# A chunked recurrence laid out by head parity: products in two opposite corners of the TensorE array

## What is computed

```python
def step(state, inp):
    r_t, w_t, k_t, v_t, a_t, b_t = inp
    sa = jnp.einsum('bhij,bhj->bhi', state, a_t)
    state = state * w_t[:, :, None, :] + sa[..., None] * b_t[:, :, None, :] + v_t[..., :, None] * k_t[:, :, None, :]
    y = jnp.einsum('bhij,bhj->bhi', state, r_t)
    return state, y
...
y = (y - mean) * lax.rsqrt(var + GN_EPS) * ln_w + ln_b
y = y + jnp.sum(rh * kh * r_k, axis=-1, keepdims=True) * vh
```

## Time and profile before

| | |
|---|---|
| median of the runs | 1049.82 us |
| span of the profiled execution | 1047.7 us |
| TensorE busy | 831.4 us (79%) |
| VectorE busy | 644.8 us (62%) |
| ScalarE busy | 390.1 us (37%) |
| GpSimd busy | 343.9 us (33%) |
| share of the chain that ended last | PE 50%, DMA 27%, DVE 12%, issue 5% |
| L880, the inversion's products | 864 records, 21.8 us busy |
| L954, L974, L984, L990 | 64 records each, 4.6, 4.6, 4.4 and 4.5 us busy |
| L964, products with the state | 48 records, 6.5 us busy |
| L873, gram products | 128 records, 4.5 us busy |

### The profile page before, as it was taken

One profiled execution on the slowest core, in us unless ns is written; L12 is line 12 of the kernel. 1 busy time (PEld: TensorE's weight loads), 2 busy tenths in 40 slices (PEclk: granted clock), 3 DMA queues, 4 the chain that ended last, 5 costly groups with the idle time before them and its releaser, 6 DMA issues.

```text
span 1047.7 us, 16371 instructions
## 1 busy us (share of the span) xinstructions
PE 831.4 (79%) x5744; PEld 488.2 (47%) x5744; DVE 644.8 (62%) x1570; ACT 390.1 (37%) x1102; POOL 343.9 (33%) x307
## 2 busy tenths in 40 slices
PE   9999999999999999766875875766666656656655
PEld 8887888788888887422422422321111111111111
DVE  4543550487343428886686686686685785785784
ACT  2025142215220102744443543444443443443443
POOL 1000000510020004445355355355445445455441
PEclk9999999999999999988888888778767667667667
DMA  8443423222223297999999999999999999999996
GB/s 347 146 149 126 160 104 134 81 82 87 78 93 111 102 415 276 425 427 427 426 427 426 426 428 426 426 426 426 426 426 428 426 428 427 427 428 427 428 426 282
DMA packets 46874, 329.66 MB, mean 315 GB/s; under 512 B 5344, under 2 KB 5600, under 8 KB 7520
## 3 DMA queue, kind: packets, MB, share of 16 engines
q0 software_dynamic: 36864, 268.45, 60.8%
q1 hardware_dynamic: 9104, 57.65, 15.2%
q10 hardware_dynamic: 848, 2.75, 0.7%
HBM read 327.78 MB, written 1.05 MB: 314 GB/s over the span
## 4 chain that ended last, share of the span: by engine, by line
PE 50%; DMA 27%; DVE 12%; issue 5%; ACT 4%; POOL 1%; POOLq 0%; DVEq 0%; ACTq 0%; SPq 0%
DMA pool_mem<-in_experts,pool_mem 27%; PE psum_proj L639 11%; PE psum_job L1100 7%; PE psum_proj L1012 7%; DVE pool_mem L2009 5%; PE psum_proj L1075 5%; PE psum_proj L1038 4%; PE psum_proj L652 3%; PE psum_job L880 2%; DVE pool_mem L1899 1%; PE psum_job L1059 1%; PE psum_proj L1059 1%; ACT pool_mem L1425 1%; DVE pool_mem L1896 1%; ACT pool_mem L1422 1%
## 5 line engine op out<-in xcount | busy, mean ns | idle before, releaser
L1100 PE MATMUL psum_job<-pool_mem 64*64 64x512 f32 x2048 | 350.9, 793 | 204.3 <-ACT pool_mem L1425 196.3
L2108 POOL DMA_INDIRECT pool_mem<-in_experts,pool_mem x256 | 309.0, 1207 | 393.4 <-PE psum_job L1100 264.0
L2009 DVE CUSTOM_DVE_ANT_0 pool_mem<-pool_mem 128x1024 f32<-128x1024 f32 x256 | 309.6, 1224 | 163.9 <-DMA pool_mem<-in_experts,pool_mem 162.7
L1100 PEld LDWEIGHTS psum_job<-pool_mem 64*64 64x64 f32 x2048 | 83.1, 162 | 452.3 <-issue 451.2
L1418 ACT ACTIVATE pool_mem<-pool_mem 128x1 f32<-128x1 f32 x256 | 51.6, 201 | 262.7 <-DVE pool_mem L2009 256.8
L639 PE MATMUL psum_proj<-pool_mem 128*128 128x256 f32 x544 | 118.9, 379 | 0.0
L639 PEld LDWEIGHTS psum_proj<-pool_mem 128*128 128x128 f32 x544 | 103.0, 190 | 15.1 <-issue 1.3
L1425 ACT ACTIVATE pool_mem<-const,pool_mem 128x64 f32<-128x64 f32 x256 | 89.1, 348 | 18.4
L1422 ACT ACTIVATE pool_mem<-pool_mem 128x1 f32<-128x1 f32 x256 | 75.4, 294 | 9.3
L1012 PE MATMUL psum_proj<-pool_mem 128*128 128x256 f32 x320 | 74.0, 384 | 0.0
L1075 PE MATMUL psum_proj<-pool_mem 128*128 128x256 f32 (+1 forms) x320 | 65.4, 360 | 4.7 <-ACT pool_mem L1454 2.5
(11 more groups left out here) (293 smaller groups left out, 858.1 us busy)
## 6 DMA issues: line engine op xcount, KB each, us to landing
pool_mem<-in_weights SPq DMA_DIRECT2D x50, 1024.0 KB, 4.9
pool_mem<-in_experts,pool_mem POOLq DMA_INDIRECT x256
pool_mem<-in_weights ACTq DMA_DIRECT2D x2, 512.0 KB, 6.4
pool_mem<-in_xT SPq DMA_DIRECT2D x2, 512.0 KB, 6.3
pool_mem<-in_memT SPq DMA_DIRECT2D x1, 1024.0 KB, 10.9
pool_mem<-in_x ACTq DMA_DIRECT2D x1, 1024.0 KB, 12.3
const<-in_const SPq DMA_DIRECT2D x1, 825.5 KB, 14.2
rows<-in_rows SPq DMA_DIRECT2D x1, 512.0 KB, 16.1
```

What stands on the lines that cost most here:

```text
L1100: ins = mm(sum_bank(t, d)[sum_strip(i, d), :], lhsT=diag[rows_, g % DIAGS, :], rhs=slot[g % SLOTS][rows_, D + 512 * d:D + 512 * d + 512], ...
L2009: ins = V.tensor_tensor_reduce(u, u, xn_tok[:, t, :], 1.0, 0.0, ALU.mult, ALU.add, hid[:, par, s_:s_ + 1])
L2108: G_.indirect_dma_start(slot[s_ % SLOTS], None, t_in["experts"], bass.IndirectOffsetOnAxis(ap=expert_i[:, par, s_:s_ + 1], axis=0)).then_i ...
```

## The change

The layout of tokens in the recurrence goes by the head's parity. Even heads have partitions 0 to 63, odd heads 64 to 127, for all chunks (`own_rows`); which of the 8 column blocks holds a head depends on chunk and head (`own_col`). Input half and output half of each product are then the same, the head's parity, and the products of heads 0, 1, 2, ... go to the corners (0, 0) and (1, 1) in turn. The state, the right-hand side and U become 128x256 each, without the zero blocks, and `from_state` becomes 8 products of 64x64x64. The gram products write to the half they read from. The copies of v, b and k are cut into four pieces each (`by_parity`), and so are Y's copy (in two) and GpSimd's product for `gn_shift`. The bonus sums become 32 small products by four columns of ones, one for each head and chunk.

```diff
--- before.py
+++ after.py
         LmT = part(Q0 + 64 * K1, HEADS, CHUNK)
         y_rwkv = part(E0, CT, S)
-        state = part(Q0 + 72 * K1, CT, P)
-        rhs_sb = part(Q0 + 74 * K1, W)
-        U = part(Q0 + 76 * K1, W)
+        state = part(Q0 + 72 * K1, CT, HD)
+        rhs_sb = part(Q0 + 74 * K1, CT, HD)
+        U = part(Q0 + 76 * K1, CT, HD)
...
             return ap.rearrange("p (a b) -> p a b", a=2)
+
+        row_halves = [slice(CHUNK * n, CHUNK * n + CHUNK) for n in range(2)]
+
+        def own_rows(h):
+
+            return row_halves[h % 2]
+
+        def own_col(n, h):
+
+            return CT * ((n + h) % 2) + h // 2
+
+        def of_parity(ap, m):
+
+            return ap.rearrange("p (a m i) -> p a m i", m=2, i=HD)[:, :, m, :]
+
+        def by_parity(dst, src):
+
+            for n in range(2):
+                for m in range(2):
+                    j = CT * ((n + m) % 2)
+                    yield dst[row_halves[m], j:j + CT, :], of_parity(src[row_halves[n]], m)
...
                 o = begin(("bonus", t))
-                for i in range(CT):
-                    ins = mm(o[:, 2 * i:2 * i + 2], lhsT=rkk[:, i, t * P:(t + 1) * P], rhs=c("headsel"),
-                             start=True, stop=True)
+                for h in range(HEADS):
+                    for n in (2 * t, 2 * t + 1):
+                        j = own_col(n, h)
+                        ins = mm(o[own_rows(h), 4 * j:4 * j + 4], lhsT=rkk[own_rows(h), h // 2, CHUNK * n:CHUNK * n + CHUNK],
+                                 rhs=ones[own_rows(h), 0:4], start=True, stop=True)
                 end(ins, ("bonus", t))
...
+            blocks = row_halves
 
             def gram_matrices(t, g):
-                for h in range(4 * g, 4 * g + 4):
-                    o = begin(("gram", t, h))
-                    b0, cc = HD * (h % 2), h // 2
+                for j in range(4 * g, 4 * g + 4):
+                    o = begin(("gram", t, j))
                     for i, src in enumerate((bb, kb)):
-                        for n in range(2):
-                            tc = slice(t * P + CHUNK * n, t * P + CHUNK * n + CHUNK)
-                            ins = mm(halves(o[blocks[n], 2 * CHUNK * i:2 * CHUNK * i + 2 * CHUNK]), lhsT=src[b0:b0 + HD, cc, tc],
-                                     rhs=ar[b0:b0 + HD, cc, :, tc], start=True, stop=True)
-                    end(ins, ("gram", t, h))
+                        for r in range(2):
+                            c0 = t * P + CHUNK * ((g + r) % 2)
+                            tc, own = slice(c0, c0 + CHUNK), row_halves[r]
+                            ins = mm(halves(o[own, 2 * CHUNK * i:2 * CHUNK * i + 2 * CHUNK]), lhsT=src[own, j % CT, tc],
+                                     rhs=ar[own, j % CT, :, tc], start=True, stop=True)
+                    end(ins, ("gram", t, j))
 
             def block_product(o, left, right, g, i, b, crossed):
 
...
 
-            def chunk_cols(n):
-
-                r0 = CHUNK * (n % 2)
-                return n // 2, slice(CHUNK * n, CHUNK * n + CHUNK), slice(r0, r0 + CHUNK)
+            def head_out(o, h):
+
+                return o[own_rows(h), (h // 2) * HD:(h // 2) * HD + HD]
 
             def chunk_rhs(n):
 
-                t, tc, tl = chunk_cols(n)
+                t = n // 2
                 if n % 2 == 0:
                     for g in range(2):
                         wait_read(pe, ("XT", t, LEVELS - 1, g))
                 o = begin(("rhs", n))
                 for h in range(HEADS):
-                    hs = slice(h * HD, (h + 1) * HD)
-                    ins = mm(o[tl, hs], lhsT=gram[tl, h, 2, :], rhs=vtok[tl, t, hs], start=(h == 0), stop=(n == 0),
+                    r, j = own_rows(h), own_col(n, h)
+                    ins = mm(head_out(o, h), lhsT=gram[r, j, 2, :], rhs=vtok[r, t, j, :], start=(h < 2), stop=(n == 0),
                              skip_group_check=True)
                 if n > 0:
                     wait_read(pe, ("S", n - 1))
-                    ins = from_state(o, 0, tl, tc, True)
+                    ins = from_state(o, 0, n, True)
                 end(ins, ("rhs", n))
 
-            def from_state(o, i, tl, tc, last):
-
-                for cc in range(CT):
-                    ins = mm(o[tl, cc * P:(cc + 1) * P], lhsT=ar[:, cc, i, tc], rhs=state[:, cc, :], start=False, stop=last,
-                             skip_group_check=True)
+            def from_state(o, i, n, last):
+
+                for h in range(HEADS):
+                    r = own_rows(h)
+                    ins = mm(head_out(o, h), lhsT=ar[r, h // 2, i, CHUNK * n:CHUNK * n + CHUNK], rhs=state[r, h // 2, :],
+                             start=False, stop=last, skip_group_check=True)
                 return ins
 
             def chunk_u(n):
 
-                t, tc, tl = chunk_cols(n)
                 o = begin(("U", n))
                 wait_read(pe, ("rhs", n))
                 for h in range(HEADS):
-                    ins = mm(o[tl, h * HD:(h + 1) * HD], lhsT=XT[tl, h, :], rhs=rhs_sb[tl, h * HD:(h + 1) * HD],
-                             start=True, stop=True)
+                    r = own_rows(h)
+                    ins = mm(head_out(o, h), lhsT=XT[r, own_col(n, h), :], rhs=rhs_sb[r, h // 2, :], start=True, stop=True)
                 end(ins, ("U", n))
 
             def chunk_y(n):
 
-                t, tc, tl = chunk_cols(n)
+                t = n // 2
                 o = begin(("Y", n))
                 for h in range(HEADS):
-                    hs = slice(h * HD, (h + 1) * HD)
-                    mm(o[tl, hs], lhsT=gram[tl, h, 3, :], rhs=vtok[tl, t, hs], start=(h == 0), stop=False, skip_group_check=True)
+                    r, j = own_rows(h), own_col(n, h)
+                    mm(head_out(o, h), lhsT=gram[r, j, 3, :], rhs=vtok[r, t, j, :], start=(h < 2), stop=False,
+                       skip_group_check=True)
                 if n > 0:
-                    from_state(o, 1, tl, tc, False)
+                    from_state(o, 1, n, False)
                 wait_read(pe, ("U", n))
                 for h in range(HEADS):
-                    hs = slice(h * HD, (h + 1) * HD)
-                    ins = mm(o[tl, hs], lhsT=gram[tl, h, 1, :], rhs=U[tl, hs], start=False, stop=True, skip_group_check=True)
+                    r = own_rows(h)
+                    ins = mm(head_out(o, h), lhsT=gram[r, own_col(n, h), 1, :], rhs=U[r, h // 2, :], start=False, stop=True,
+                             skip_group_check=True)
                 end(ins, ("Y", n))
                 if n < NCHUNK - 1:
                     o = begin(("S", n))
-                    for last, src, with_ in ((False, ktok[:, t], vtok[:, t]), (True, btok[:, t], U)):
-                        for h in range(HEADS):
-                            hs, r = slice(h * HD, (h + 1) * HD), slice(HD * (h % 2), HD * (h % 2) + HD)
-                            ins = mm(o[r, (h // 2) * HD:(h // 2 + 1) * HD], lhsT=src[tl, hs], rhs=with_[tl, hs],
-                                     start=(not last and h < 2), stop=last, skip_group_check=True)
+                    for h in range(HEADS):
+                        r, j = own_rows(h), own_col(n, h)
+                        mm(head_out(o, h), lhsT=ktok[r, t, j, :], rhs=vtok[r, t, j, :], start=(h < 2), stop=False,
+                           skip_group_check=True)
+                    for h in range(HEADS):
+                        r = own_rows(h)
+                        ins = mm(head_out(o, h), lhsT=btok[r, t, own_col(n, h), :], rhs=U[r, h // 2, :], start=False, stop=True,
+                                 skip_group_check=True)
                     end(ins, ("S", n))
 
...
                 wait_job(act, ("vt", t))
-                job_read(nc.scalar.copy(vtok[:, t, :], bank(("vt", t))), ("vt", t))
+                for to, new in by_parity(vtok[:, t], bank(("vt", t))):
+                    ins = nc.scalar.copy(to, new)
+                job_read(ins, ("vt", t))
...
                     for i in range(1, N_GATE0):
                         sigmoid_gate("gate0", i)
             for t in range(TILES):
                 wait_job(act, ("bonus", t))
-                job_read(nc.scalar.copy(sm(BON + 8 * t, 8), bank(("bonus", t))[:, 0:8]), ("bonus", t))
+                job_read(nc.scalar.copy(sm(BON + 8 * t, 8), bank(("bonus", t))[:, 0:32].rearrange("p (a b) -> p a b", b=4)[:, :, 0]),
+                         ("bonus", t))
...
 
+            def head_cols(job):
+
+                return bank(job)[:, 0:CT * HD].rearrange("p (a b) -> p a b", a=CT)
+
             def chunk_copy(job, n, dst):
-                tl = slice(CHUNK * (n % 2), CHUNK * (n % 2) + CHUNK)
                 if (job, n) == ("rhs", 0):
                     act.wait_ge(sg["cleared"], 1)
                 wait_job(act, (job, n))
-                job_read(nc.scalar.copy(dst[tl, :], bank((job, n))[tl, :]), (job, n))
+                job_read(nc.scalar.copy(dst, head_cols((job, n))), (job, n))
+
```

(26 more changed lines are left out.)

16 lines of the change are left out of this document (8 added, 8 removed).

## The result

The changed kernel took **1044.32 us** (median of 5 runs, 1042.4 to 1045.82) against 1049.86 (5 runs, 1049.78 to 1057.03): ratio of the runs 0.9932, 95% interval 0.9912 to 0.9952. The two medians are 5.5 us apart, and the ratio, over all runs, is worth 7.1 us. The forecast was 1042.7, with 1039 to 1047 as range and "within 1%" as the likeliest case; both hold. The profiled execution (1044.32 us, span 1042.5) is 5.2 us shorter than the one of before, where 7.1 had been forecast, and this difference is the part worth explaining. A launch lasts 1.8 us longer than its profiled span (1044.32 to 1042.5), so, by the same distance, the execution of before with a span of 1047.7 us lasted about 1049.5, less than each of its five runs.

The account below looks back on a forecast made before the run. The kernel was taken as two parts in series, TensorE's list of work, then the expert gathers, bound by transfers. Terms -7.5 - 3.8 + 0.2 + 3.5 + 0.5 = -7.1 us gave 1042.7 us, range 1039 to 1047.

Parts of the forecast that it names:

- One-corner sets: Recurrence: 16 sets (part of `rhs`, `U`, two parts of `Y`) fall from 0.94 to 0.47 us each: -7.5 us.
- State products: Recurrence: 4 products of 128x128 become 8 of 64x64, each of six saving 0.55 plus 0.08 us changeover: -3.8 us.
- State update: Recurrence, S: 32 records in two corners before and after, so 0.
- The chain of chunk 0: TensorE stalls of 0.2 us after U and 0.3 after S, against one of 0.3 before: net +0.2 us.
- Gram: Gram products use two corners instead of four, +0.87 us for each of four groups: +3.5 us.
- Bonus: Bonus sums become 32 small products, 64 records, 2.2 us against 1.7: +0.5 us.
- ScalarE and GpSimd: More, smaller copies and `gn_shift` pieces were to cause no TensorE wait: 0, with 1.4 us left at GpSimd's worst end.
- One for one to the end: TensorE time removed between 150 and 357 us should arrive at the end, unless another engine becomes late.
- (a): Rival: gram costs nothing, so -10.6 us, 1039.2; chance 0.06.
- (b): Rival: opposite corners writing the same bank take turns, so +14.6 us, 1064; chance 0.05.
- (c): Rival: dearer helpers (bonus +2.4, GpSimd pieces over 1.4 us, other small stalls), so -3.2 us, 1046.6; chance 0.13.
- (d): Rival: the gain stops before the end because the gathers start by something other than TensorE, 1049.8; chance 0.03.

Follow-up runs that it names:

- Experiment 1: Changed kernel with each set's heads grouped, four even then four odd, instead of alternating: 1048.61 us, ratio 0.996 to the kernel before.
- Experiment 2: Changed kernel with every other gram product's inputs read from the other row half, so four corners (output not the reference's): 1039.04 us, ratio 0.9874 to before.
- experiment 3: Changed kernel with 32 records of the `up` projection done twice, adding TensorE work: 1051.16 us, ratio 0.999 to the kernel before.
- experiment 7: Changed kernel unaltered, run again on the chip of the kernel before: 1043.87 us against 1051.39, ratio 0.9929.
- experiment 6: Kernel before, with three unread products put into TensorE's idle stretch ahead of the first queries of tile 1: 1050.61 us, ratio 0.9991 to before.
- experiment 4: Changed kernel with output half by parity of chunk and head, gram in four corners, bonus as before the change: 1042.98 us, ratio 0.9901 to before.
- Experiment 9: Four-corner variant with three unread products in TensorE's idle stretch, plus two sets moved to cover waits in the recurrence: 1041.24 us.

## Why the prediction came out right, step by step

- **One-corner sets, -7.5.** Right: 0.47 us a set, with both corners on one bank and products that accumulate. What the forecast couldn't know from the trace of before, that accumulation doesn't order the two corners, holds. Experiment 1 adds that 4.4 us hang on the order within the sets, those of the state products and of the state update among them.
- **State products, -3.8.** Right in size: 0.47 us (283.46 to 283.93) instead of 1.02.
- **State update, 0.** Right: still two sets of 16 at 0.47 each (275.11 to 276.04).
- **The chain of chunk 0, stalls of 0.2 and 0.3.** Right: they are 0.25 and 0.26.
- **Gram, +3.5.** Nearly right: it is 0.81 a group instead of 0.87, 3.2 in all. Experiment 2 gets 3.07 back by the four corners alone.
- **Bonus, +0.5.** It is 0.28. A record came to 31 ns, as forecast (1.99 / 64), but the changeovers are inside it. No run measured this term at the gather by itself.
- **ScalarE and GpSimd, 0.** Right: no new wait of TensorE for either but the one for U (two for ScalarE, of 0.6 and 0.4 us, stand in both traces); the slack in front of the inversion was 4.9 us, not the 1.4 of the worst end. The 1.2 us a piece of that end had been misread: it is the mean of two records, of 0.73 and 1.59 us, and the other two of that line in the trace of before took 0.73 as well.
- **The sum.** For the forecast -7.1 us the traces have -7.13 behind chunk 3 and -7.33 at the first gather.
- **One for one to the end.** This is the step that was too simple. It holds for TensorE time up to the gather (experiments 2 and 3: 3.07 and 6.98 us) and for executions alike in clock: experiment 7's has the forecast span, 1040.6. But an execution may lose 1.0 to 1.2 us or more where the clock falls at the first queries of tile 1, and 0.9 us more if its last products run at half clock. The profiled one of before had neither, the first one of after had both. I had kept one execution's distance to its median, 2.1 us, as a constant, where 1.8 is what a launch has around its span, and read the spread of 1049.78 to 1057.03 as nothing that bears on a difference of 7. That the first median, 1044.32, came within 1.6 us of the forecast is partly luck: five runs on each side, spread over 3.4 and 7.3 us.

**The rivals.** (a), gram free, fell with 0.81 us a group. (b), opposite corners on one bank taking turns, fell: sets at 0.47. The rule that the forecast named for it, from the Trainium skill, TensorEngine Tiling (Array Packing), section Restrictions and Gotchas, would have kept them at 0.94; the traces of both kernels speak against it for products with different output partitions. (c), dear helpers, fell: 0.6 us a piece, bonus +0.3. (d), a gain that stops before the end, is not it either, though 2.1 us were missing in the first comparison: they were lost at two places behind the gather, both at half clock, and are back in an execution without either (experiment 7). With the runs side by side on one chip 7.5 us arrive, with the place filled 7.4.

**Shown, and not shown.** That the two corners carry the gain and that gram's price is its corners is shown by experiments 1 and 2 at the first gather. That filling the idle stretch narrows the spread is shown for the kernel before, on one chip (experiment 6); for the changed kernel the six filled runs all lie below six of the eleven unfilled ones, but on different chips. That the clock's fall is what makes the long runs is not shown: only single executions were traced, the kernel before never with the fall, a fall cost 1.0 us at the last dot product between the two executions of the changed kernel, and the long runs of before lie up to 6.3 us above the shortest. What decides from one execution to the next whether the clock falls there stays open: the start of the stretch and TensorE's work ahead of it are the same. Other falls further on remain, and why experiments 3 and 4 lost another 1.0 and 1.4 us before the last dot product was not traced. Experiment 9's second part took 648.1 us although its stretch was filled; at least 0.9 of that is the half clock of its last products.

## What to carry to other kernels

Small products that shared one corner of the array took twice the time of the same products in two opposite corners: alternate them, product by product and not in groups, and check what else then loses corners (gram here gave back 3.2 of 10.6 us). Add up TensorE's list only as far as the next part starts, compare that mark in the two traces, and compare what is behind it separately: here the sum agreed with the first mark to 0.2 us while the total was off by 2. Split that second part once more before naming one cause: 0.9 of those 2 us were the last products of the kernel. Where runs spread by several microseconds, look for an idle stretch of TensorE followed by a fall of its clock; three idle products in such a stretch narrowed the spread here from 6.3 to 1.8 us, while the median moved by 0.8 us, not clear of noise. And a short wait is not worth covering with a set that must then enter and leave the tiled form by itself.
